# Two turns of attention taken together on TensorE in the second mixer of a two-network kernel

## What is computed

```python
def dense_attention(q, k, v, scale):
    ...
    def block(qi):
        s = jnp.einsum("bhqd,bhkd->bhqk", qi, kf) * scale
        return jnp.einsum("bhqk,bhkd->bhqd", jax.nn.softmax(s, axis=-1), vf)
    o = lax.map(block, qb)
    ...
def mixer_ab(...):
    ...
    kb = jnp.concatenate([kv[..., :B_NOPE], jnp.broadcast_to(k_pe, (B, S, B_HEADS, B_ROPE))], axis=-1)
    vb = kv[..., B_NOPE:]
    out_b = dense_attention(qb, kb, vb, (B_NOPE + B_ROPE) ** -0.5).astype(x.dtype)
    return jnp.concatenate([out_a, out_b], axis=-1) @ w_out
```

## Time and profile before

| | |
|---|---|
| median of three runs | 2400.43 us (2400.34 to 2401.1) |
| profiled execution | 2400.3 us, its span 2398.3 us |
| TensorE busy | 2366.4 us, 99% of the span |
| GpSimd busy | 1886.6 us, 79% |
| VectorE busy | 1172.2 us, 49% |
| ScalarE busy | 707.6 us, 30% |
| granted clock of TensorE, mean | 0.999 |
| B's attention on TensorE | from 185.0 us (first scores) to 249.8 us (end of the last values) |

### The profile page before, as it was taken

How to read it: one execution, slowest core, us unless ns; L and a number is a source line. 1 busy time by engine, 2 the same in 40 slices (tenths; PEclk the granted TensorE clock), 3 DMA queues, 4 the chain that set the end, 5 groups by cost and what they waited for, 6 DMA issues and landing times.

```text
span 2398.3 us, 32491 instructions
## 1 busy us (share of the span) xinstructions
PE 2366.4 (99%) x11204; PEld 1856.2 (77%) x11204; DVE 1172.2 (49%) x1625; ACT 707.6 (30%) x1281; POOL 1886.6 (79%) x1565
## 2 busy tenths in 40 slices
PE   9999999999999999999999999999999999999998
PEld 7755788888878765788888778777888888778887
DVE  4686443332281777633342496656222666662224
ACT  3166242330031445333220135244010252440101
POOL 8711798889889765998888898837999988369996
PEclk9999999999999999999999999999999999999999
DMA  5200222222223110232222233211322232113222
GB/s 191 80 26 27 70 88 97 96 96 96 97 70 115 62 53 28 88 105 96 96 96 96 79 111 115 87 45 62 105 97 96 88 115 88 45 62 102 100 96 88
DMA packets 58862, 207.01 MB, mean 86 GB/s; under 512 B 6544, under 2 KB 9104, under 8 KB 58512
## 3 DMA queue, kind: packets, MB, share of 16 engines
q1 hardware_dynamic: 57472, 201.31, 25.0%
q10 hardware_dynamic: 1296, 4.39, 0.5%
HBM read 203.58 MB, written 2.10 MB: 86 GB/s over the span
## 4 chain that ended last, share of the span: by engine, by line
PE 88%; DVE 5%; POOL 4%; issue 2%; ACT 1%; DMA 1%; POOLq 0%; DVEq 0%; SPq 0%
PE bank L795 24%; PE bank L797 24%; PE bank L796 24%; PE bank L853 4%; PE bank L904 2%; PE bank L937 2%; PE bank L965 2%; POOL w_both L3014 2%; PE bank L908 1%; POOL w_both L3017 1%; PE bank L1030 1%; PE bank L1074 1%; DVE work L2225 1%; DMA ring<-in_weights 1%; PE bank L912 1%
## 5 line engine op out<-in xcount | busy, mean ns | idle before, releaser
L3014 POOL TENSOR_TENSOR w_both<-ring,unit 128x512 fp32r<-128x512 f32 x690 | 782.6, 1134 | 366.4 <-PE bank L797 250.1
L3017 POOL TENSOR_TENSOR w_both<-ring,w_both 128x512 fp32r<-128x512 f32 x690 | 934.2, 1354 | 54.0
L795 PE MATMUL bank<-moving_hi,w_both 128*128 128x512 f32 x1834 | 719.5, 392 | 9.3 <-POOL w_both L3017 2.8
L796 PE MATMUL bank<-moving_lo,w_both 128*128 128x512 f32 x1834 | 714.0, 389 | 0.0
L797 PE MATMUL bank<-moving_hi,w_both 128*128 128x512 f32 x1834 | 714.0, 389 | 0.0
L795 PEld LDWEIGHTS bank<-moving_hi,w_both 128*128 128x128 f32 x1834 | 344.0, 188 | 96.7 <-issue 17.1
L797 PEld LDWEIGHTS bank<-moving_hi,w_both 128*128 128x128 f32 x1834 | 344.1, 188 | 72.4
L796 PEld LDWEIGHTS bank<-moving_lo,w_both 128*128 128x128 f32 x1834 | 344.2, 188 | 70.3 <-issue 0.7
L2959 DVE TENSOR_TENSOR region<-region,bank 128x512 f32<-128x512 f32 x64 | 39.7, 682 | 280.5 <-PE bank L797 280.5
L2111 ACT ACTIVATE region<-bank 128x512 f32<-128x512 f32 x64 | 38.3, 598 | 364.5 <-PE bank L797 364.4
L795 PE MATMUL bank<-hid_hi,w_both 128*128 (+1 forms) x352 | 137.7, 391 | 0.0
(11 more groups left out here) (396 smaller groups left out, 3753.2 us busy)
## 6 DMA issues: line engine op xcount, KB each, us to landing
ring<-in_weights SPq DMA_DIRECT2D x374, 512.0 KB, 3.2
out<-region SPq DMA_DIRECT2D x8, 256.0 KB, 2.2
x<-in_x_t SPq DMA_DIRECT2D x3, 512.0 KB, 7.7
region<-in_tables ACTq DMA_DIRECT2D x1, 1312.0 KB, 6.7
region<-in_tables ACTq DMA_DIRECT2D x1, 1024.0 KB, 5.1
region<-in_p_t ACTq DMA_DIRECT2D x2, 512.0 KB, 5.4
ring<-in_weights SPq DMA_DIRECT2D x2, 256.0 KB, 4.7
x<-in_x_t ACTq DMA_DIRECT2D x2, 256.0 KB, 4.9
```

The lines of the kernel that those rows point to most:

```text
L795: pe.matmul(bank, lhs[0], rhs[0], start=start, stop=False, skip_group_check=True)
L796: pe.matmul(bank, lhs[0], rhs[1], start=False, stop=False, skip_group_check=True)
L3014: pool.tensor_tensor(w_parts[0][:, s, at], ring[:, s, at], unit[:, 0:1].broadcast_to([P, BLK // 2]), ALU.mult).then_inc(split_hi, 1)
L3017: pool.tensor_tensor(w_parts[1][:, s, at], ring[:, s, at], w_parts[0][:, s, at].bitcast(F32), ALU.subtract).then_inc(split_ready, 1)
```

## The change

B's call of `heads_in_pairs` gets `together=2`; A's keeps 1.

```diff
                 heads_in_pairs([u for u in UNITS if u[0] == kind], q, k, v, lambda u: [],
                                last_rope=("qkA", 6) if kind == "A" else None, opened=opened,
                                second=before_second if kind == "B" else None,
-                               between=last_keys if kind == "A" else values_stored)
+                               between=last_keys if kind == "A" else values_stored, together=1 if kind == "A" else 2)
```

## The result

| | us |
|---|---|
| kernel before, median of 8 runs | 2400.39 (2399.94 to 2401.39) |
| changed kernel, median of 8 runs | 2407.36 (2407.26 to 2408.69) |
| difference | +6.97 |
| ratio | 1.003, 95% interval 1.0021 to 1.0039 |
| span of the profiled execution | 2405.4, against 2398.3 before |

The change makes the kernel slower by 0.3%. TensorE's busy time has hardly moved; its waits have grown, and they stand in the second mixer's attention.

What follows compares the result with a forecast made beforehand. TensorE, without waits in B's steady attention, was taken as the bound. Start 2.1, middle 4.7 and end 0.2 us sum to 7.0, so 2400.43 becomes 2407.4 us; range +5.0 to +9.0 us, chance 0.80.

Steps and rivals of the forecast that it cites:

- What bounds the stage: B's attention: TensorE busy 42.87 of 42.90 us, nothing running ahead behind it, so the whole shift of 7.0 us goes through.
- start, to the scores of turn 6: B's first turns: scores 3 ahead of transposes 0 delay scores 6 from 205.24 to 207.3, a loss of 2.1 us.
- middle, five pairs: B's turns 4 to 13: a pair takes 8.55 us against 7.60, +0.95 each, +4.7 us.
- end, from transposes 14: B's last pair, without scores: +0.5 us, less 0.26 us because values cover a copy, together +0.2 us.
- The copy wait: B's pairs: second transposes wait for ScalarE's copy to free banks 4 and 5; starts 2.18 us apart, 1.21 us waiting.
- The joins: B's pairs: joining scores saves 0.11 us and joining values 0.15 us, together 0.26 us a pair.
- (a): B's pairs: the waits hide and only the joins remain, about 2 us saved, 2398.5 us; chance 0.04.
- (b): B's start loses less, or unseen slack swallows some: +3 to +4.8 us, 2403.4 to 2405.2; chance 0.06.
- (c): B's pairs: ScalarE becomes the pace, scores wait for exponentials, 0.5 us in six pairs, 2410.4 us; chance 0.07.
- (d): B's attention: the clock falls to 1.2 GHz for the whole stage, +58 us, some 2466 us; chance 0.03.

Runs made afterwards that it cites:

- e5_pairs_at_start: Kernel before, with only turns 0 to 3 of B taken in pairs and turns 4 to 15 singly: 2402.34 us.
- e1: Changed kernel, with the values of each turn in B put back behind that turn's own transposes: 2401.95 us.
- e3: Changed kernel, with ScalarE's copy of the transposed rows issued twice in a row in B: 2422.59 us.
- e8: Changed kernel, with ScalarE's copy split into one instruction per bank and each bank handed back by itself: 2401.95 us.
- e4: Kernel before, with ScalarE's copy of the transposed rows issued twice in a row in B: 2403.23 us.
- e10: Changed kernel, with ScalarE's copy doubled in B as in e3 and each turn's values behind its own transposes as in e1: 2419.72 us.
- e2_again: The same kernel as e2_scores_between, run again with more runs: 2398.19 us.
- e2_scores_between: Changed kernel, with scores in B put back between the two sets of transposes and only values joined; last pair as before: 2398.26 us.
- e9: The order of e2_scores_between in both mixers, A and B, where that run had it in B alone: 2399.37 us.
- e6: Kernel before, with pairs in the first mixer (A) and B left single: 2406.65 us.

## Why the prediction was right

**What bounds the stage.** Right. TensorE had no wait in B's steady part, nothing ran ahead behind it, and the shift went through whole: the first L795 stands 7.15 us later, the span is 7.1 us longer, the median 6.97.

**The sum.** Its three pieces against the rows of the trace after:

| | predicted | measured |
|---|---|---|
| start, to the scores of turn 6 | +2.1 | 207.17 - 205.24 = +1.9 |
| middle, five pairs | +4.7 | (250.12 - 207.17) - 38.03 = +4.9 |
| end, from transposes 14 | +0.2 | (256.95 - 250.12) - (249.80 - 243.27) = +0.3 |
| sum | +7.0 | +7.15 |

In a pair: scores 3.53 us predicted and 3.53 measured (210.70 - 207.17); transposes to transposes 2.18 and 2.16; the second transposes, which now stand behind a wait, 0.97 and 1.02 (213.88 - 212.86); values 1.87 and 1.88. The pair is 8.59 us and not 8.55, and that is most of what the middle was short of. The start was built from more guesses than the rest and came out right. Counted from the scores of turn 2 (191.28 before, 191.08 after) it costs 2.1 us and not 1.9, since this execution happened to reach the stage 0.2 us earlier, and e5_pairs_at_start has it alone at 2.1. By the same count the stage is 7.35 us longer. When the stage is reached differs by 0.9 us between the executions in which nothing ahead of it was changed (190.90 to 191.82), so the agreement of 6.97 with 7.0 to 0.03 us is luck; this pair of traces gives 7.1 to 7.4.

One thing in the text on the range doesn't fit. Forecast were +5.0 to +9.0, which is 2405.4 to 2409.4 us; the sentence that has it reach from 2404.8 to 2410.4 describes +4.4 to +10.0, and its own terms give neither end (4.7 + 0.2 = +4.9 below, 7.0 + 1.8 + 0.9 = +9.7 above). The measured time lies in the middle of both.

**The copy wait.** Right, by three different edits: it shrinks under values (e1), it grows with the copy by 1.05 us (e3, 2.16 to 3.21 from transposes to transposes), and it falls to 0.25 us with a hand-over by bank (e8), while the same doubled copy costs the old order nothing in its steady part (e4).

**The joins.** Scores joined save 0.11 us in a pair, as taken: 3.53 us for two where one takes 1.82. Values joined save 0.14 (two of 1.01 against 1.88). The Trainium skill ("TensorE: Matmul & The Clock Gate", Part 2, "Step-by-step: what each phase is for") has TensorE load weights early when the row groups don't conflict, or when the load goes to the background weight buffer. If that had hidden everything at these borders, nothing would have been saved and the sum, by my estimate, would have been 8.8; the trace after decides for the rows. That doesn't contradict the page: weights of 96 and of 128 rows share rows, so its first condition isn't met here, and no run shows whether the second is. What I undersized is the gain where values are joined and scores stay between: 0.34 and not 0.15 us in a pair, since I counted one border of the values and there are three.

**The rivals.** (a) didn't come: the joins save 0.25 us where they would have needed 1.2. (b) didn't come. (c) didn't come in the changed kernel: ScalarE's last exponentials of a pair end 5.7 us after the first transposes start, and the second scores start at about 6.8. Its wait came in e10, with 1.06 us more on ScalarE a turn. (d) didn't come either, but for a thinner reason than I gave. I argued that a wait of 1.78 us in A had left the clock at 1.00. In the trace of e3, where A is untouched, TensorE's rows at the same wait are these:

```profile
123.78 1.84 PE L965 MATMUL bank<-tabs,work 128*128 128x128 f32 x8 [1.77 <-DVE work L2211]
125.56 1.93 PE L937 MATMUL bank<-region 128*64 128x256 f32 x8
```

They took 1.06 and 1.08 us in the kernel before. This wait of 1.77 to 1.78 us stands in eleven of the traces, and behind it the clock fell in two, e3 and e2_again (transposes of 1.90 us), though not in e2_scores_between, which is the same kernel as e2_again. So one execution with the clock at 1.00 didn't show that such a wait is safe. The chance of 3% was right in outcome; the evidence for it was one draw.

## What to carry to other kernels

Before several steps are batched by kind, ask what each step's output buffer waits for: with one set of banks, whatever stands between two uses hides the emptying, and taking it away exposes what is left of producer plus copy (2.16 us here) once the producer's own work (0.97) is taken off. Join only those steps that aren't the cover; here scores between the transposes and joined values give 7.26 us a pair, against 7.60 singly and 8.59 fully batched. The same argument gains where other matmuls stand between, so read the cover in each stage, and read whether an engine sets the pace from waits, not from its busy share.

## What the runs showed of the hardware that I had not expected

TensorE's granted clock fell to its lower level, 1.2 GHz, behind single waits ahead of a set of transposes. Waits of 1.11 to 1.20 us never did it, in the changed kernel, e4 or the steady part of e10. In e3, with 2.17 us (once 2.21) of idleness between two sets of transposes, it fell in four of eight places and stayed in the others; behind the one wait of 2.17 us in e10, 2.79 us in e9 and 3.81 us in e6 it fell too; behind 1.77 to 1.78 us it fell in two of eleven traces, and in those two A took 59.8 us and not 59.1. Where it fell, sixteen matmuls of values took 2.5 to 3.5 us and not 1.95, and a pair of e3 lost 1.5 to 1.6 us on top of its wait. What decides in the cases between isn't settled by these runs.

Changing between kinds of matmul has a price that depends on the neighbour: the eight transposes take 0.88 us when scores follow and 0.97 when values follow, the four matmuls of scores 1.72 us behind transposes and 1.82 behind values.
